# A decoder block in one kernel: the bias broadcast in sixteen pieces on the weight queue, and the first two probability turns inside the dense product ahead of them

## The reference, cut to what matters

```python
o_a = mla(mla_q_lat, mla_kv_lat, mla_k_rope, positions, ..., w_uq, w_ukv)
o_b = dsa(dsa_q, dsa_k, dsa_v, idx_q, idx_k, idx_w, tab_dsa)
o_c = nsa(nsa_q, nsa_kc, ..., nsa_gate, ..., tab_nsa)
gates = jax.nn.sigmoid(branch_gate.reshape(B, S, N_BRANCH, D_MODEL))
merged = (gates[:, :, 0] * (o_a @ w_branch[l, 0]) + gates[:, :, 1] * (o_b @ w_branch[l, 1])
          + gates[:, :, 2] * (o_c @ w_branch[l, 2]))
x = x + rmsnorm(merged @ w_out[l], g[NORM_POST_MIX])
```

## Time and profile before

| | before |
|---|---|
| median of 3 runs | 1622.41 us (1621.66 to 1624.34) |
| the profiled execution | 1619.99 us, its span 1618.2 us |
| TensorE matmuls busy | 1505.1 us, 93% of the span |
| VectorE, ScalarE busy | 699.4 us, 573.4 us |
| DMA queue of SP (q1) | 126.17 MB, 24.6% of 16 engines |
| DMA queue of POOL (q0) | 12.58 MB, 4.3% |
| mean granted TensorE clock | 0.979 |

### The profile page before, as it was taken

The page is one execution under the profiler, slowest core; times in us unless marked ns, Lnnn a source line. Parts: engine busy times, 40 slices in busy tenths (PEclk is TensorE's granted clock), DMA queues, the critical chain, the costliest instruction groups (busy, mean ns, idle before and its releaser), DMA issues.

```text
span 1618.2 us, 17357 instructions
## 1 busy us (share of the span) xinstructions
PE 1505.1 (93%) x7230; PEld 1195.9 (74%) x7230; DVE 699.4 (43%) x1126; ACT 573.4 (35%) x879; POOL 185.8 (11%) x133
## 2 busy tenths in 40 slices
PE   6995999999999999899999999999995999999995
PEld 5853677887887888776766887796763888888884
DVE  4563555755233325555255443852227332222334
ACT  4452452214234223435355234443343332133221
POOL 1000000012110100000000111322214110011011
PEclk9997999999999999899999999999997999999997
DMA  5229222332221233721100332351120223323311
GB/s 174 85 32 125 69 92 65 104 105 65 92 78 53 79 112 100 225 79 39 53 27 27 133 122 84 99 162 53 52 78 26 89 93 104 104 81 102 104 53 52
DMA packets 133852, 140.43 MB, mean 87 GB/s; under 512 B 6899, under 2 KB 129008, under 8 KB 133776
## 3 DMA queue, kind: packets, MB, share of 16 engines
q1 hardware_dynamic: 130496, 126.17, 24.6%
q0 software_dynamic: 2992, 12.58, 4.3%
q10 hardware_dynamic: 288, 0.59, 0.1%
HBM read 131.99 MB, written 7.34 MB: 86 GB/s over the span
## 4 chain that ended last, share of the span: by engine, by line
PE 81%; DVE 8%; ACT 5%; DMA 4%; issue 1%; POOL 0%; SPq 0%; ACTq 0%; DVEq 0%
PE dense L578 22%; PE dense L580 22%; PE dense L579 22%; PE score L691 3%; PE score L710 3%; PE attended L710 3%; DMA raw<-in_mla_w_uq 2%; DVE weight_low L1481 2%; PE turned L691 1%; DVE y L1838 1%; ACT probsT L1085 1%; ACT weight_high L1085 1%; PE turned L703 1%; PE score L681 1%; DVE probs L1640 1%
## 5 line engine op out<-in xcount | busy, mean ns | idle before, releaser
L1486 DVE TENSOR_TENSOR weight_low<-raw,weight_high 128x2048 fp32r<-128x2048 f32 (+2 forms) x105 | 226.6, 2164 | 442.6 <-ACT weight_high L1085 442.5
L578 PE MATMUL dense<-hidden_high,weight_high 128*128 128x512 f32 x808 | 317.3, 393 | 10.3 <-POOL hidden_low L1992 7.9
L580 PE MATMUL dense<-hidden_high,weight_low 128*128 128x512 f32 x808 | 315.3, 390 | 0.0
L579 PE MATMUL dense<-hidden_low,weight_high 128*128 128x512 f32 x808 | 315.1, 390 | 0.0
L1085 ACT ACTIVATE weight_high<-raw 128x2048 fp32r<-128x2048 f32 (+4 forms) x151 | 224.1, 1504 | 217.6 <-PE dense L580 176.5
L578 PEld LDWEIGHTS dense<-hidden_high,weight_high 128*128 128x128 f32 x808 | 152.2, 188 | 43.6 <-issue 8.1
L580 PEld LDWEIGHTS dense<-hidden_high,weight_low 128*128 128x128 f32 x808 | 152.1, 188 | 31.9
L579 PEld LDWEIGHTS dense<-hidden_low,weight_high 128*128 128x128 f32 x808 | 152.3, 188 | 31.5 <-issue 0.2
L578 PE MATMUL dense<-up_high,weight_high 128*128 128x512 f32 x256 | 99.6, 389 | 0.0
L579 PE MATMUL dense<-up_low,weight_high 128*128 128x512 f32 x256 | 99.6, 389 | 0.0
L580 PE MATMUL dense<-up_high,weight_low 128*128 128x512 f32 x256 | 99.6, 389 | 0.0
(11 more groups left out here) (309 smaller groups left out, 2447.1 us busy)
## 6 DMA issues: line engine op xcount, KB each, us to landing
raw<-in_w_in SPq DMA_DIRECT2D x34, 1024.0 KB, 5.2
raw<-in_mlp_w SPq DMA_DIRECT2D x32, 1024.0 KB, 5.2
raw<-in_w_branch SPq DMA_DIRECT2D x12, 1024.0 KB, 5.1
raw<-in_nsa_cmp_w SPq DMA_DIRECT2D x8, 1024.0 KB, 5.6
raw<-in_cross_wkv SPq DMA_DIRECT2D x8, 1024.0 KB, 5.5
bias_scratch<-bias_row POOLq DMA_DIRECT2D x1, 5120.0 KB, 55.2
raw<-in_w_in SPq DMA_DIRECT2D x9, 512.0 KB, 5.0
bias_strips<-bias_scratch POOLq DMA_DIRECT2D x8, 512.0 KB, 4.0
```

The lines of the kernel that those rows point to most:

```text
L578: pe.matmul(out_ap, ah, bh, start=first, stop=False)
L579: pe.matmul(out_ap, ah, bl, start=False, stop=False)
L580: return pe.matmul(out_ap, al, bh, start=False, stop=last)
L1486: ins = V.tensor_tensor(dst, src, hi.bitcast(F32), ALU.subtract)
```

## The change

It has two parts.

The bias broadcast leaves POOL's queue. SP issues it as sixteen DMAs, each with one partition of `biasRow` as its source, and two of them behind each of the eight MLA slabs. Ahead of the first of these slabs SP waits for the setup product to be taken out of PSUM, since that writes `biasRow`. POOL's wait for `scratch` counts sixteen DMAs.

```diff
-            for s in range(2, slab_at["cw", 0, 0]):
+            for s in range(2, slab_at["uq", 0]):
+                load(s)
+            sp.wait_ge(taken["V"], taken_count[product_at["setup"]])
+            for s in range(slab_at["uq", 0], slab_at["uq", 0] + 8):
+                load(s)
+                for h in range(2 * (s - slab_at["uq", 0]), 2 * (s - slab_at["uq", 0]) + 2):
+                    sp.dma_start(scratch[h:h + 1], biasRow[h:h + 1, :].unsqueeze(1).broadcast_to((1, P, T + P))).then_inc(scratch_written, 16)
+            for s in range(slab_at["uq", 0] + 8, slab_at["cw", 0, 0]):
                 load(s)
...
-            pool.wait_ge(taken["A"], taken_count[product_at["m1", 0]])
-            pool.dma_start(scratch, biasRow[:, :].unsqueeze(1).broadcast_to((16, P, T + P))).then_inc(scratch_written, 16)
...
-            pool.wait_ge(scratch_written, 16)
+            pool.wait_ge(scratch_written, 16 * 16)
```

```diff
-                late_one = None
+                turns, values = [], []
                 for att, parts in heads:
                     for n, (unit, probs_of, i0, rows, value) in enumerate(parts):
-                        turn_tile(unit, probs_of, i0, rows, m)
-                        if late_one:
-                            value_tile(*late_one)
-                        late_one = (att, n == 0, n == len(parts) - 1, value, i0, rows, m)
+                        turns.append((unit, probs_of, i0, rows, m))
+                        values.append((att, n == 0, n == len(parts) - 1, value, i0, rows, m))
                         m += 1
-                value_tile(*late_one)
+
+                def begin(n):
+
+                    turn_tile(*turns[n])
+
+                def finish():
+
+                    for n, value in enumerate(values):
+                        value_tile(*value)
+                        if n + 2 < len(turns):
+                            turn_tile(*turns[n + 2])
+                return begin, finish
+
+            def ahead(begin, chunks):
+
+                def at_chunk(k):
+                    if k >= chunks - 2:
+                        begin(k - chunks + 2)
+                return at_chunk
...
+                if p:
+                    begin, finish = mla_values(p - 1)
                 t_mode(s, two(g), [lambda t, k: wide(t, 2, 512)[:, k, 0:P], lambda t, k: wide(t, 2, 512)[:, k, 256:384]],
-                       2, (latH[:, 3:5, :], latL[:, 3:5, :])).then_inc(product_ready, 1)
+                       2, (latH[:, 3:5, :], latL[:, 3:5, :]), ahead(begin, 2) if p else None).then_inc(product_ready, 1)
                 if p:
-                    mla_values(p - 1)
+                    finish()
...
+            def turned_begin(heads, m):
+
+                rows = [t for _, tiles in heads for t in tiles]
+                for k in range(2):
+                    act.wait_ge(turned_ready, m + k + 1)
+                    copy(probsT[0:rows[k][0], (m + k) % 3, 0:rows[k][1]],
+                         TURNED[(m + k) % 2][0:rows[k][0], 0:rows[k][1]]).then_inc(probsT_ready, 1)
+
...
                 ready(("m2", p))
                 high(s + 2)
+                before = [(2 * (p - 1) + h, causal) for h in range(2)]
+                if p:
+                    turned_begin(before, 8 * (p - 1))
                 ready(("m3", p))
                 copy(kT[:, :, :], bank(("m3", p))[:, :, :]).then_inc(taken["A"], 1)
                 if p:
-                    turned([(2 * (p - 1) + h, causal) for h in range(2)], 8 * (p - 1))
+                    turned(before, 8 * (p - 1))
...
```

More of the change, by code:

```diff
@@ L692, in score_tile, with attention @@
                 mm.then_inc(score_ready, 1)
-            def attend(heads, m):
+            def attention(heads, m):
                 def turn_tile(unit, probs_of, i0, rows, m):
@@ L737, in mla_values @@
             def mla_values(p):
-                attend([(2 * p + h, causal_parts(2 * p + h, h, lambda j, h=h: vN[:, j, h * P:(h + 1) * P]))
+                return attention([(2 * p + h, causal_parts(2 * p + h, h, lambda j, h=h: vN[:, j, h * P:(h + 1) * P]))
                         for h in range(2)], 8 * p)
@@ L783, in merge @@
             def merge(b, last_values):
+                begin, finish = last_values
                 for n in range(GROUPS):
@@ L788, in merge @@
                     free(g)
-                    t_mode(slab_at["bg", b, n], two(g), both, KD, hT).then_inc(product_ready, 1)
+                    t_mode(slab_at["bg", b, n], two(g), both, KD, hT, None if n else ahead(begin, KD)).then_inc(product_ready, 1)
                     if n == 0:
-                        last_values()
+                        finish()
                     g = product_at["bp", b, n]
@@ L795, in merge @@
                            lambda k: pe.wait_ge(attended_taken, 8 * b + k + 1)).then_inc(product_ready, 1)
-            merge(0, lambda: mla_values(3))
+            merge(0, mla_values(3))
             def dsa_values(p):
-                attend([(8 + 2 * p + h, causal_parts(8 + 2 * p + h, h, lambda j, h=h: vN[:, j, h * P:(h + 1) * P]))
+                return attention([(8 + 2 * p + h, causal_parts(8 + 2 * p + h, h, lambda j, h=h: vN[:, j, h * P:(h + 1) * P]))
                         for h in range(2)], 32 + 8 * p)
@@ L809, in _ @@
             for p in range(4):
+                if p:
+                    begin, finish = dsa_values(p - 1)
                 for name in ("dq", "dk"):
@@ L812, in _ @@
                     free(g)
-                    t_mode(slab_at[name, p], two(g), both, KD, hT).then_inc(product_ready, 1)
+                    t_mode(slab_at[name, p], two(g), both, KD, hT,
+                           ahead(begin, KD) if p and name == "dk" else None).then_inc(product_ready, 1)
                 if p:
-                    dsa_values(p - 1)
+                    finish()
                 else:
@@ L827, in _ @@
             pe.wait_ge(taken["A"], taken_count[product_at["dv", 3]])
-            merge(1, lambda: dsa_values(3))
+            merge(1, dsa_values(3))
             for name in ("kc", "vc"):
@@ L882, in nsa_values, with features @@
                     heads.append((16 + 2 * p + h, parts))
-                attend(heads, 64 + 18 * p)
-            def features(name, i):
+                return attention(heads, 64 + 18 * p)
+            def features(name, i, at_chunk=None):
                 g = product_at[name, i]
                 free(g)
-                t_mode(slab_at[name, i], two(g), both, KD, hT).then_inc(product_ready, 1)
+                t_mode(slab_at[name, i], two(g), both, KD, hT, at_chunk).then_inc(product_ready, 1)
             def nsa_v(r):
@@ L906, in _ @@
                 if p:
-                    features("nq", p)
+                    begin, finish = nsa_values(p - 1)
+                    features("nq", p, None if p == 2 else ahead(begin, KD))
                     if p == 2:
-                        features("kk", r)
-                    nsa_values(p - 1)
+                        features("kk", r, ahead(begin, KD))
+                    finish()
                     if p == 2:
@@ L931, in _ @@
                     pe.wait_ge(taken["A"], taken_count[product_at["vv", r]])
-            merge(2, lambda: nsa_values(3))
+            merge(2, nsa_values(3))
             pe.wait_ge(x2_loaded, 16)
@@ L1186, in exps @@
                 ins.then_inc(exp_done, 1)
+            def turned_begin(heads, m):
[4 more added lines that the diff above has]
+                         TURNED[(m + k) % 2][0:rows[k][0], 0:rows[k][1]]).then_inc(probsT_ready, 1)
             def turned(heads, m):
+                begun = m + 2
                 def head_out(att):
@@ L1196, in turned @@
                     for n, (rows, cols) in enumerate(tiles):
-                        act.wait_ge(turned_ready, m + 1)
-                        copy(probsT[0:rows, m % 3, 0:cols], TURNED[m % 2][0:rows, 0:cols]).then_inc(probsT_ready, 1)
+                        if m >= begun:
+                            act.wait_ge(turned_ready, m + 1)
+                            copy(probsT[0:rows, m % 3, 0:cols], TURNED[m % 2][0:rows, 0:cols]).then_inc(probsT_ready, 1)
                         m += 1
@@ L1226, in merge @@
             def merge(b, tiles, first_tile):
+                heads = [(8 * b + 6 + h, tiles) for h in range(2)]
+                turned_begin(heads, first_tile)
                 for n in range(GROUPS):
@@ L1233, in merge @@
                     if n == 0:
-                        turned([(8 * b + 6 + h, tiles) for h in range(2)], first_tile)
+                        turned(heads, first_tile)
                     high(slab_at["bg", b, n] + 2)
@@ L1251, in _ @@
                 if p:
-                    turned([(8 + 2 * (p - 1) + h, causal) for h in range(2)], 32 + 8 * (p - 1))
+                    before = [(8 + 2 * (p - 1) + h, causal) for h in range(2)]
+                    turned_begin(before, 32 + 8 * (p - 1))
+                    turned(before, 32 + 8 * (p - 1))
                 high(slab_at["dk", p] + 2)
```

(6 more changed lines are left out.)

## The result

The changed kernel takes 1659.44 us (median of 4 runs, 1659.3 to 1662.28), the kernel before, measured with it, 1622.04 us. The ratio is 1.0233, with a 95% interval from 1.0215 to 1.025: 37.4 us slower. The forecast was slower, with 1683 us.

What follows compares the result with a forecast made beforehand. TensorE sets the end, through dense lines 578 to 580, 22% each. Profiled 1619.99 us + 66.4 for the longer MLA stage - 5.6 for the turns = 1680.8, with 2.4 to the median 1683; own range 1659 to 1725, with rivals 1590 to 1725.

Steps and rivals of the forecast that it cites:

- The turns: First two turns move ahead of the dense product's last two chunks; TensorE's short waits at line 710 go, 7.3 us.
- What happens to the queue: In the MLA stage slabs stand behind pieces on SP's queue; stage 66.4 us longer, the old 20.64 us replaced.
- The rate of a piece: One-partition piece out of SBUF runs at a quarter of 105 GB/s, 26.2 GB/s; a pair takes 25.0 us, 22 to 31.
- a door: Narrow place on the source side that several SBUF partitions share; sixteen partitions sit behind four or five, one behind one.
- The slabs' share of the queue: Each later MLA slab occupies SP's queue: 1.5 us for `uq`, 1.3 for `ukv`, 2.6 for `("bg", 0, 0)`.
- The start of the queue: SP issues the first slab, `("uq", 0)`, at 61.17; it lands 4.4 us later, data through at about 64.6.
- From the slab to the end: `("bg", 0, 0)` lands at 278.0, pair 3's first value product at 280.5, then 2.27 us for TensorE's lower clock.
- Rival A: Everything hides: pieces at 47 GB/s or more, a pair under 14 us, time 1594 us; chance 0.16.
- Rival C: Each source partition gives only its share of the rate: a pair takes 100 us, time 2283 us; chance 0.05.
- rival E: A slab passes the pieces on SP's queue; with none to three slabs late 1594 to 1656 us; chance 0.03.
- Rival D: Pieces go through one engine at 21.9 GB/s, a pair 30 us, time 1723 us; inside the forecast's range, no own chance.
- Where it flips: Time of a pair of pieces below which everything hides in the MLA stage, 13.9 us; whole gain spent at 17.5 us.

Runs made afterwards that it cites:

- four_adjacent: Changed kernel with four DMAs instead of sixteen pieces, one behind each slab `("ukv", p)`, each reading four neighbouring partitions, 4p to 4p + 3: 1687.04 us, one run.
- four_apart: Changed kernel with four DMAs instead of sixteen pieces, each reading partitions p, p + 4, p + 8 and p + 12: 1594.91 us, one run.

## Why the prediction was right in kind and 24 us too high

- **The turns**: right in mechanism and size. Eleven waits, 7.3 us, were priced; alone the part gave 7.5 us. The cover of the third copy held: no wait of TensorE for it appears. The new wait in front of the turns did show in the MLA stage of after, 4.0 us once and 1.7 us in two waits, where the stage hung on the queue anyway; in the kernels with only the turns or with the DRAM source no turn waits.
- **What happens to the queue**: right. Slabs behind pieces, ScalarE held up in `high`, TensorE in line 715, and the old wait of 20.64 us replaced, not added. The late slabs are the ones that were named, with 10.13, 17.45 and 17.96 us of idle TensorE for `("uq", 2)`, `("uq", 3)` and `("bg", 0, 0)`.
- **The rate of a piece**: 26.2 GB/s was taken, 27.0 is measured (12.12 us). Eight pairs at 24.24 instead of 25.0 us are 6 us less. The working took a door to be as wide as what one engine draws, 21.9 GB/s, which gave 4.8 doors; a door is wider than that, and the quarter that was chosen between a fifth and 30 GB/s was a choice, not a result of the sum. The Trainium skill's 27.2 GB/s (SBUF — State Buffer, "Door 1: The DMA port swizzle") was the better number, and its map of which partitions share a port is what the four_adjacent and four_apart kernels show: 0 to 3 one port, 0, 4, 8 and 12 four.
- **The slabs' share of the queue**: the step that failed, "Each later slab occupies the queue at some 400 GB/s ... 1.5 us ... 1.3 us ... 2.6". Those 12.3 us were added to the eight pairs. Measured, a slab adds -0.5 us, since its packets pass beside the pieces. The queue from the first slab's data to `("bg", 0, 0)` took about 8 x 23.7 = 190 us, not 212.3: 6 us by the rate, 16 us by the slabs.
- **The start of the queue**: 61.17 in the profile of before, 63.57 in that of after, 62.6 to 64.6 in the others. It hides 2.4 us of the error: the gate slab was forecast at 278.0 and read at 257.83, which is 22.5 us less by the queue and 2.4 us more by the start. The first late slab, `("ukv", 0)`, was forecast at 91.9 and read at 91.93: that is luck, since a rate and a slab term that are too slow and a start that is too early cancel there.
- **From the slab to the end**: forecast as 2.5 us from the slab to the value product, it took 260.28 - 257.83 = 2.45. The lower clock showed as forecast: the first two matmuls take 2.07 us, as in the first row, against 1.12 before. It showed three times instead of once, since two earlier stalls have it too, but there the next slab's arrival sets the end. From that product to the first dense matmul of the gate it took 282.49 - 260.28 = 22.21 us, before 235.77 - 216.28 = 19.49: 2.7 us more, where 2.27 were added.
- **The rest of the 24 us**: the gate slab is 20.2 us of them. The forecast also added 2.4 us because the median of before stood above its profiled execution; in the changed kernel the two agree (1659.44 and 1659.58). The turns gave 6.8 us here instead of 5.6.
- **ScalarE's waits**: five for slabs were forecast; the trace has seven.
- **Rival A** (everything hides) was the right picture for another kernel: it gave 1594 us, and with the DRAM source the time is 1591.5. Its reason, the DRAM side of the broadcast, is refuted. **Rival C** (share by partition) and **rival E** (slabs pass) are refuted: C by the rate, E by the 27.6 us in which the median `uq` slab lands and the 23.70 us between slabs. Slab packets do pass pieces, but a slab lands only with its last packet. **Rival D** (one engine) is refuted by the 90.6% busy share of sixteen engines.
- **Where it flips**: 13.9 us were worked out, 15.2 to 15.4 us of cadence measured. The slab term, which isn't there, explains most of it: without the 12.3 us the same sum gives (189 - 64.6 - 1) / 8 = 15.4, and 15.1 with the measured start.

## What to carry to other kernels

Before a broadcast out of SBUF is cut up or moved, look at how many partitions it reads and which: its rate is set there, and a small source makes a long transfer, however many engines carry it. If the source is small, write it to DRAM once and replicate from there; here that alone turned 37 us lost into 30 us won. On an in-order queue the price of what is put in between is flat up to the free time of a slab and then the whole excess for each slab, so work out that corner first.

## What the runs showed of the hardware that was not expected

- A transfer of 576 KB costs the queue nothing (-0.5 us) when it stands between slow pieces on all sixteen engines. The packets of 128 to 138 us show slab and pieces moving at once. My reading, which was not tested, is that engines finish a slow piece at different times and those that are early carry slab packets. Beside a broadcast on about four engines three quarters of a slab pass, and what is left costs at most 1.5 us.
- SP's issue instruction is held up by the transfers in front: 12.7 us for two pieces, 11.4 us for a slab, 0.4 to 0.6 us each where the pieces are fast. Whatever SP had to issue next would have been late too, on any buffer.
- One piece read by all sixteen engines and four rows read by about four engines run at 27 and 25 GB/s: it makes little difference how many engines wait at one door.
